# Token chunks of 512, 512 and 128 in place of three of 384 in the gate and merge products of a hybrid encoder step

## The chip, the cores and the metric

The kernel runs on one core of a Trainium2 chip. The metric is the device time of one execution in microseconds (us). The profile comes from one execution of its own, whose time stands in the table below beside its span, which runs from the first to the last instruction.

Engines are named as the profile names them: PE is TensorE's matmul, PEld its weight load, DVE VectorE, ACT ScalarE, POOL GpSimd, SP SyncE, which issues the transfers. All matrix products that matter here have 32-bit operands in the format `float32r` (fp32r in the rows of ACT and DVE; the rows of PE print it as f32, as they do for plain 32-bit floats).

## What is computed

One layer of a streaming encoder, for 1024 new tokens behind 16 learned meta tokens and for 8 running streams of 16 tokens, model width 1024. The input projection gives ten parts of 1024 columns; attention has 8 heads of 128. Cut to the parts that the change touches:

```
xn = rmsnorm(x, norm_g);  p = xn @ w_in + b_in
B, C, h, z_c, q, k, v, z_s, g_c, g_s = split(p)
y_c = silu(z_c) * (B * causal_conv3(C * h))
y_s = silu(z_s) * stick_breaking(q, k, v)
m   = sigmoid(g_c) * (y_c @ w_conv_o) + sigmoid(g_s) * (y_s @ w_sb_o)
y   = x + m @ w_o
```

The meta tokens need no output, so everything from the gates on covers 1152 tokens: 1024 of the prompt and 128 of the running streams.

## The kernel before

Activations lie turned, 128 channels on the partitions and tokens along the free axis. A weight matrix is taken in tiles of 1024 input channels by 128 output channels. For near-32-bit accuracy both operands of a product are split in a high and a low part in fp32r, and `split_product` (L64) issues three matmuls for each of the 8 blocks of 128 input channels: high by high (L70), low activation or low weight (L71, L72). A weight tile therefore needs 24 matmuls for each chunk of tokens, and each of these matmuls has a weight load of 128 columns of its own. A chunk fills one PSUM bank, of which 384 of the 512 columns are used; three chunks, `CHL` (L48), cover the 1152 tokens, so a tile takes 72 matmuls.

The program is four stages, one behind the other, each engine with a program written out by hand and semaphores between them:

- the front: norm, then the short convolution, eight blocks of four weight tiles (`conv_chunk`, L385; its first two tiles use chunks of 400, 384 and 384 tokens, since they hold the meta tokens too, the other two `CHL`)
- the gates (`two_blocks`, L438 on PE, L527 on ACT, the loop at L651 on DVE): eight blocks of three weight tiles, g_c, then y_c @ w_conv_o, then g_s. Chunk n goes into bank `g_banks[n]` (L246). ACT takes sigmoids out of the banks (L538, L548), DVE multiplies (L656), and both results go to memory
- attention, eight heads
- merge and output (`merge_and_output`, L1472), over `LIVE_CHUNKS` (L49): eight tiles of w_sb_o, in which DVE multiplies (L1603), adds (L1605) and takes the low part (L1596) while ACT takes the high part (L1569); then eight tiles of w_o, whose result ACT copies out (L1579), PE turns back (L1655) and DVE adds to x (L1616)

`LIVE_CHUNKS` also cuts the last head's output at the seam between attention and merge (L1348, L1437, L1444). The gates of the attention heads (`silu_gate`, L1039) use `CHL`.

PE waits for a weight tile (`ready`) and, before each chunk, until the chunk before it in the same bank has been read. Weight tiles are loaded two ahead, split by ACT (L148) and POOL (L153) after the product that used the slot.

Of the kernel before, what the change touches and what calls it, by code (L numbers as in the profile page):

```python
# [34 lines left out]
META, SEQ, NB, DS, PAST = 16, 1024, 8, 16, 512  # L35
HEADS, HD = 8, 128
PT = SEQ // P
SAMPLE0 = META + SEQ
TOK = SAMPLE0 + NB * DS
# [6 lines left out]
OFF = {n: i * D for i, n in enumerate(["B", "C", "h", "z_c", "q", "k", "v", "z_s", "g_c", "g_s"])}  # L46
CH = [(0, META + 384), (META + 384, META + 768), (META + 768, TOK)]
CHL = [(META, META + 384), (META + 384, META + 768), (META + 768, TOK)]  # L48
LIVE_CHUNKS = [(a - META, e - META) for a, e in CHL]  # L49


def tile_cols(t):
# [47 lines left out]
def hold(eng, sem, value):  # L100


    eng.wait_ge(sem, value)
    eng.sem_inc(HELD["waits_held"], 1)
# [59 lines left out]
def x_moving(c, c0, c1):  # L164
    return (lambda k: c.xh[:, k, c0:c1], lambda k: c.xl[:, k, c0:c1])
# [8 lines left out]
def front(c, d):  # L174
# [81 lines left out]
    def bias(name, i):  # L256
        return c.bias[:, bass.ds(i + OFF[name] // P, 1)]
# [114 lines left out]
    def tensor(pe):  # L372
        def turn(p):

            n = rows[p]
            pe.wait_ge(normed, p + 1)
            for j in range(2):
                if p >= 2:
                    pe.wait_ge(lo_ok, 2 * (p - 2) + j + 1)
                for k in range(4):  # L380
                    mm = pe.transpose(x_banks[p % 2][j][:, k * P:k * P + n],
                                      xn[0:n, p % 3, (4 * j + k) * P:(4 * j + k + 1) * P], c.ident[0:n, 0:n])
                mm.then_inc(turned, 1)

        def conv_chunk(i, j, n, ks=range(KC)):  # L385
            c0, c1 = (CH if names[j] in "Ch" else CHL)[n]
            q = 3 * j + n
            if q < 2:
                pe.wait_ge(d_out, 9 * i + q + 1)
            elif q < 5:  # L390
                pe.wait_ge(c_out, 3 * i + q - 1)
            else:
                pe.wait_ge(d_out, 9 * i + q - 4 + 2)
            mm = w.product(pe, j, banks[q % 2][:, 0:c1 - c0], x_moving(c, c0, c1), ks)
            if KC - 1 in ks:
                mm.then_inc(full, 1)

        pe.wait_ge(made, 4)
        pe.wait_ge(gain_in, 16)
        for j in range(2):  # L400
            mm = pe.matmul(c.bank_z[:, j * 512:(j + 1) * 512], ones[:, :], gb[:, j * 512:(j + 1) * 512],
                           start=True, stop=True)
        mm.then_inc(gain_ok, 1)
        for p in range(TILES):
            turn(p)
            if p == 4:
                pe.wait_ge(small_in, 48)
                pe.transpose(small_bank[:, 0:80], b80[:, :], c.ident[0:80, 0:80])
                for k in range(KC):
                    pe.transpose(small_bank[:, 80 + 3 * k:83 + 3 * k], cw3[:, k * P:(k + 1) * P], c.ident[0:3, 0:3])  # L410
                for k in range(KC):
                    mm = pe.transpose(small_bank[:, 128 + 16 * k:144 + 16 * k], st16[:, k * P:(k + 1) * P],
                                      c.ident[0:16, 0:16])
                mm.then_inc(small_turned, 1)
            if p in C_HALVES:

                n, ks = C_HALVES[p]
                if n == 0:
                    w.ready(pe, 0, 0)
                pe.wait_ge(lo_ok, 2 * CHUNK_TILES[n])  # L420
                conv_chunk(0, 0, n, ks)
        pe.wait_ge(lo_ok, 2 * CHUNK_TILES[2])
        conv_chunk(0, 0, 2)
        for j in range(1, 4):
            w.ready(pe, 0, j)
            for n in range(3):
                conv_chunk(0, j, n)
        with pe.Fori(1, KC) as i:
            for j in range(4):
                w.ready(pe, i, j)  # L430
                for n in range(3):
                    conv_chunk(i, j, n)
        pe.wait_ge(last_ok, 2 * KC)
        for k in range(KC):
            mm = pe.transpose(c.bank_z[0:18, k * P:(k + 1) * P], last[:, k, :], c.ident[:, :])
        mm.then_inc(last_turned, 1)

        def two_blocks(i, first):  # L438
            for j in range(6):
                b = 2 * i + j // 3  # L440
                wg.ready(pe, i, j)
                for n, (c0, c1) in enumerate(CHL):
                    if j % 3 == 0:
                        if first and j == 0 and n == 2:
                            pe.wait_ge(last_out, 1)
                        pe.wait_ge(s_ok, 3 * b + n + 1)
                    elif j % 3 == 1:
                        if first and j == 1 and n == 0:
                            pe.wait_ge(yl_ok, 3 * KC)
                        pe.wait_ge(g_ok, 3 * b + n + 1)  # L450
                    else:
                        pe.wait_ge(m_ok, 3 * b + n + 1)
                    right = x_moving(c, c0, c1) if j % 3 != 1 else (
                        lambda k: yh[:, k, c0 - META:c1 - META], lambda k: yl[:, k, c0 - META:c1 - META])
                    wg.product(pe, j, g_banks[n][:, 0:c1 - c0], right).then_inc(g_full, 1)

        two_blocks(0, True)
        with pe.Fori(1, KC // 2) as i:
            two_blocks(i, False)

    def scalar(act, first_splits):
# [65 lines left out]
        def two_blocks(i, more):  # L527
            for b in range(2):
                m = 2 * i + b

                def split(j):
                    if b == 0 or more or j < 3:
                        jj = 3 * b + j
                        wg.split_hi(act, *((i, jj) if jj < 6 else (i + 1, jj - 6)))

                for n, (c0, c1) in enumerate(CHL):
                    hold(act, g_full, 9 * m + n + 1)
                    act.activation(gate[:, c0 - META:c1 - META], g_banks[n][:, 0:c1 - c0], ACT.Sigmoid,  # L538
                                   bias=bias("g_c", m)).then_inc(g_ok, 1)
                split(2)  # L540
                act.wait_ge(g_full, 9 * m + 6)
                split(3)
                if b and not more:
                    first_splits(act)
                act.wait_ge(s_stored, 16 * m + 16)
                for n, (c0, c1) in enumerate(CHL):
                    hold(act, g_full, 9 * m + 6 + n + 1)
                    act.activation(outs[:, 1, c0 - META:c1 - META], g_banks[n][:, 0:c1 - c0], ACT.Sigmoid,  # L548
                                   bias=bias("g_s", m)).then_inc(s_ok, 1)
                split(4)  # L550

        act.wait_ge(yl_ok, 3 * KC)
        with act.Fori(0, KC // 2 - 1) as i:
            two_blocks(i, True)
        two_blocks(KC // 2 - 1, False)

    def vector(dve):
# [35 lines left out]
        with dve.Fori(0, KC) as i:  # L593
            dve.tensor_copy(us[:, :, 0:2], state[:, bass.ds(i, 1), :].rearrange("p o (b j) -> p (o b) j", j=2)
                            ).then_inc(u_ok, 1)
            for n, (c0, c1) in enumerate(CH):
# [3 lines left out]
                e = min(c1, SAMPLE0)  # L600
# [35 lines left out]
            for n, (c0, c1) in enumerate(CHL):  # L636
                q = 9 + n
                a, b = c0 - META, c1 - META
# [11 lines left out]

        with dve.Fori(0, KC) as i:  # L651
            dve.wait_ge(m_stored, 16 * i + 16)
            for n, (c0, c1) in enumerate(CHL):
                dve.wait_ge(g_full, 9 * i + 3 + n + 1)
                dve.wait_ge(g_ok, 3 * i + n + 1)
                dve.tensor_tensor(outs[:, 0, c0 - META:c1 - META], g_banks[n][:, 0:c1 - c0],  # L656
                                  gate[:, c0 - META:c1 - META], ALU.mult).then_inc(m_ok, 1)
# [16 lines left out]
    done.y_c_used, done.stored = y_c_used, all_stored  # L674
    done.conv_banks_read, done.gate_banks_read = conv_banks_read, gate_banks_read
    return Programs(sync, gpsimd, tensor, scalar, vector), done


# [79 lines left out]
def attention(c, d, buf, front_stored, following):  # L758
# [51 lines left out]
    def turn_bank(h, plan, key):  # L810

        n = plan[key]
        return FIRST_T + NT * h + n, c.bank_t[n % 2]
# [395 lines left out]
    def scalar(act):  # L1209
# [88 lines left out]
        def head(h, par, pairs, nxt, nxt2):  # L1298
# [48 lines left out]
            else:  # L1347
                for n, (a, e) in enumerate(LIVE_CHUNKS):  # L1348
                    act.wait_ge(y_ok, HEADS + n)
# [15 lines left out]
    def vector(dve):  # L1365
# [53 lines left out]
        def head(h, par, pairs, nxt, nxt2):  # L1419
# [16 lines left out]
            dve.wait_ge(t_out, turn_bank(h, plan, ("o", 1))[0] + 1 + 2)  # L1436
            for a, e in [(0, LIVE)] if nxt else LIVE_CHUNKS:  # L1437
                dve.tensor_tensor(ot[:, a:e], zs[:, a:e], ot[:, a:e], ALU.mult).then_inc(y_ok, 1)
# [4 lines left out]
            else:  # L1443
                for n, (a, e) in enumerate(LIVE_CHUNKS):  # L1444
                    dve.wait_ge(yh_ok, HEADS + n)
# [26 lines left out]
def merge_and_output(c, d, e):  # L1472
# [26 lines left out]
    turn_banks = [c.bank_t[0], c.bank_t[1], c.bank_z[:, 0:512]]  # L1499
    chunks = LIVE_CHUNKS  # L1500

# [300 lines left out]
```

## Time and profile before

| | |
|---|---|
| median of 3 executions | 1709.81 us (1708.9 to 1711.69) |
| the profiled execution | 1708.88 us, of it span 1707.1 us |
| PE busy | 1669.0 us, 98% of the span |
| DVE, ACT, POOL busy | 572.7, 516.2, 360.2 us |
| gates | about 437 to 738 us of the span |
| merge, output | about 1491 to 1592, 1592 to 1707 us |

A matmul's record begins when it starts in the array and ends when its last result is out, so records of a dense stream overlap: what one costs is the distance between the starts of neighbours, not the length of a record. Two passes of one plain 32-bit product are two records.

### The profile page before, as it was taken

Reading aid. Unit: us, or ns where it says so; the run is one execution under the profiler, and the core shown is the slowest. Engines: PE = TensorE matmul, PEld = TensorE weight load, DVE = VectorE, ACT = ScalarE, POOL = GpSimd, SP = SyncE. Lnnn points to the kernel's source line nnn. Section 1 sums busy time; section 2 is a strip of 40 time slices with the busy share of each in tenths; the row PEclk is TensorE's granted clock in tenths of the full one; section 3 lists DMA queues with packets and bytes.
Section 4 is the critical chain, followed back from the end, with each engine's and each line's share of the span. In section 5 each row is a group of like instructions: output and inputs, shape, how many; then the busy total and the mean of one; then the engine's idle time right before and its main releaser. Section 6 shows DMA issues by size and latency. Waiting matters only on the chain.

```text
span 1707.1 us, 27313 instructions
## 1 busy us (share of the span) xinstructions
PE 1669.0 (98%) x10845; PEld 1592.3 (93%) x10845; DVE 572.7 (34%) x912; ACT 516.2 (30%) x1225; POOL 360.2 (21%) x334
## 2 busy tenths in 40 slices
PE   7999999999999999999999999999999998699998
PEld 6999999999999999998999899898989897499998
DVE  5433323433200000023444343535343534544211
ACT  6211222211211111124434343434353533511111
POOL 3211212211212112132121212112121210511111
PEclk9999999999999999999999999999999999799999
DMA  5111111101222212243242423333242223434244
GB/s 165 46 30 49 48 38 37 45 29 49 65 67 79 77 65 71 83 137 92 68 117 66 119 74 97 99 89 104 83 104 76 66 63 100 157 122 157 52 129 119
DMA packets 227891, 142.15 MB, mean 83 GB/s; under 512 B 8150, under 2 KB 220710, under 8 KB 227804
## 3 DMA queue, kind: packets, MB, share of 16 engines
q1 hardware_dynamic: 227804, 140.94, 28.5%
q8 instruction: 61, 1.00, 0.2%
q14 instruction: 26, 0.21, 0.0%
HBM read 112.98 MB, written 27.93 MB: 83 GB/s over the span
## 4 chain that ended last, share of the span: by engine, by line
PE 94%; ACT 2%; DMA 1%; issue 1%; DVE 1%; POOL 1%; SPq 0%; DVEq 0%; ACTq 0%; POOLq 0%
PE bank_p L70 18%; PE bank_p L71 18%; PE bank_p L72 18%; PE bank_o L1116 4%; PE bank_z L1064 4%; PE bank_o L71 3%; PE bank_o L70 3%; PE bank_o L72 3%; PE bank_z L71 3%; PE bank_z L70 3%; PE bank_z L72 3%; PE bank_t L1105 2%; PE bank_s L71 2%; PE bank_s L70 2%; PE bank_s L72 2%; PE bank_t L1077 2%
## 5 line engine op out<-in xcount | busy, mean ns | idle before, releaser
L70 PE MATMUL bank_p<-x_hi,w_hi 128*128 128x384 f32 (+1 forms) x768 | 262.1, 341 | 2.1 <-DVE x_lo L571 1.4
L72 PE MATMUL bank_p<-x_hi,w_lo 128*128 128x384 f32 (+1 forms) x768 | 260.4, 339 | 0.0
L71 PE MATMUL bank_p<-x_lo,w_hi 128*128 128x384 f32 (+1 forms) x768 | 260.2, 339 | 0.0
L153 POOL TENSOR_TENSOR w_lo<-w_raw,w_hi 128x1024 fp32r<-128x1024 f32 x56 | 139.5, 2490 | 551.7 <-ACT w_hi L148 551.7
L70 PE MATMUL bank_p<-wqkv_hi,x_hi 128*128 128x384 f32 (+1 forms) x640 | 218.3, 341 | 0.0
L72 PE MATMUL bank_p<-wqkv_hi,x_lo 128*128 128x384 f32 (+1 forms) x640 | 211.7, 331 | 0.0
L71 PE MATMUL bank_p<-wqkv_lo,x_hi 128*128 128x384 f32 (+1 forms) x640 | 211.5, 330 | 0.0
L70 PEld LDWEIGHTS bank_p<-x_hi,w_hi 128*128 128x128 f32 x768 | 144.2, 188 | 4.3 <-DVE x_lo L571 2.6
L72 PEld LDWEIGHTS bank_p<-x_hi,w_lo 128*128 128x128 f32 x768 | 144.2, 188 | 0.0
L71 PEld LDWEIGHTS bank_p<-x_lo,w_hi 128*128 128x128 f32 x768 | 144.0, 188 | 0.0
L1395 DVE TENSOR_TENSOR_SCAN one_minus_beta<-one_minus_beta 128x1040 f32<-128x1040 f32 (+8 forms) x72 | 116.1, 1613 | 49.0 <-ACT one_minus_beta L1233 49.0
L962 POOL TENSOR_SCALAR qk_meansq<-qk_sumsq 128x2 f32<-128x2 f32 x80 | 15.3, 191 | 502.9 <-ACT squares L1214 502.9
L71 PEld LDWEIGHTS bank_p<-wqkv_lo,x_hi 128*128 128x128 f32 (+1 forms) x640 | 114.5, 179 | 1.3
L70 PEld LDWEIGHTS bank_p<-wqkv_hi,x_hi 128*128 128x128 f32 (+1 forms) x640 | 114.3, 179 | 1.1
L72 PEld LDWEIGHTS bank_p<-wqkv_hi,x_lo 128*128 128x128 f32 (+1 forms) x640 | 114.1, 178 | 1.3
L148 ACT ACTIVATE w_hi<-w_raw 128x1024 fp32r<-128x1024 f32 x56 | 59.1, 1055 | 166.2 <-PE bank_p L72 89.9
L1385 DVE SCALAR_TENSOR_TENSOR qk_rows<-qk_rows,qk_rstd,qk_gain 128x128 f32<-128x128 f32 (+1 forms) x152 | 63.8, 459 | 119.7 <-POOL qk_rstd L964 119.7
L1116 PE MATMUL bank_o<-a_turned,v_rows 128*128 128x128 f32 x576 | 80.9, 278 | 0.0
L1064 PE MATMUL bank_z<-qk_turned 128*128 128x512 f32 (+1 forms) x192 | 78.6, 519 | 1.7 <-ACT beta L1233 1.7
L1376 DVE TENSOR_TENSOR qk_rows<-bank_p,bias_qkv 128x256 f32<-128x256 f32 x80 | 32.8, 410 | 137.6 <-PE bank_p L72 135.8
L656 DVE TENSOR_TENSOR gates_out<-bank_o,gate_c 128x384 f32<-128x384 f32 x8 | 4.5, 558 | 211.9 <-PE bank_o L72 211.9
L153 POOL TENSOR_TENSOR wm_lo<-wm_raw,wm_hi 128x1024 fp32r<-128x1024 f32 x16 | 41.2, 2579 | 161.4 <-ACT wm_hi L148 161.4
(232 smaller groups left out, 3449.9 us busy)
## 6 DMA issues: line engine op xcount, KB each, us to landing
w_raw<-in_w_in SPq DMA_DIRECT2D x48, 512.0 KB, 3.8
cache_k_rows<-in_cache_k SPq DMA_DIRECT2D x64, 256.0 KB, 3.8
cache_v_rows<-in_cache_v SPq DMA_DIRECT2D x64, 256.0 KB, 4.6
wqkv_raw<-in_w_in SPq DMA_DIRECT2D x24, 512.0 KB, 5.3
m_part_scratch<-gates_out SPq DMA_DIRECT2D x8, 576.0 KB, 2.8
gate_scratch<-gates_out SPq DMA_DIRECT2D x8, 576.0 KB, 2.8
gate_s<-gate_scratch SPq DMA_DIRECT2D x8, 576.0 KB, 3.9
m_part<-m_part_scratch SPq DMA_DIRECT2D x8, 576.0 KB, 5.0
```

What stands on the lines that cost most here:

```text
L70: pe.matmul(out, lh(k), rh(k), start=k == 0, stop=False)
L71: pe.matmul(out, lh(k), rl(k), start=False, stop=False)
L72: mm = pe.matmul(out, ll(k), rh(k), start=False, stop=k == KC - 1)
L148: act.activation(self.hi[:, s, :, :], self.raw[:, s, :, :], ACT.Copy).then_inc(self.hi_ok, 1)
L153: pool.tensor_tensor(self.lo[:, s, :, :], self.raw[:, s, :, :], self.hi[:, s, :, :].bitcast(F32), ALU.subtract).then_inc(self.lo_ok, 1)
L1064: pe.matmul(c.bank_z[:, a:e], q, qk[:, par, 1, skip + a:skip + e], start=True, stop=e < w)
L1077: mm = pe.transpose(bank[:, q * P:(q + 1) * P], kc[:, j % 2, q, :], c.ident[:, :])
L1105: mm = pe.transpose(bank[0:n, m * P:(m + 1) * P], src, c.ident[:, :])
L1116: mm = pe.matmul(c.bank_o[:, 0:P], v[:, par, t, :], a, start=g == 0 and m == 0, stop=g == len(groups) - 1 and m == len(groups[g]) - 1)
L1376: dve.tensor_tensor(qkn[0:n, s, a:2 * P], bank[0:n, a:2 * P], bias3[0:n, a:2 * P], ALU.add).then_inc(rows_ok, 1)
L1385: mm = dve.scalar_tensor_tensor(out=qkn[0:n, s, j * P:(j + 1) * P], in0=qkn[0:n, s, j * P:(j + 1) * P], scalar=rs[0:n, s, j:j + 1], in1=ga ...
L1395: dve.tensor_tensor_scan(young_first, young_first, young_first, 1.0, ALU.mult, ALU.bypass).then_inc(scan_ok, 1)
```

## The change

A new list `WIDE` cuts the 1152 tokens in two chunks of 512 and one of 128. The gate products and what reads their banks take it in place of `CHL`, and `LIVE_CHUNKS` follows from it, so that the merge and output products and the seam behind the last head are cut in the same way. `CHL` itself stays for the convolution and for the attention heads' gates. The number of chunks, the banks, the semaphores and their counts stay as they were.

```diff
-LIVE_CHUNKS = [(a - META, e - META) for a, e in CHL]
+WIDE = [(META, META + 512), (META + 512, SAMPLE0), (SAMPLE0, TOK)]
+LIVE_CHUNKS = [(a - META, e - META) for a, e in WIDE]
...
                 wg.ready(pe, i, j)
-                for n, (c0, c1) in enumerate(CHL):
+                for n, (c0, c1) in enumerate(WIDE):
...
-                for n, (c0, c1) in enumerate(CHL):
+                for n, (c0, c1) in enumerate(WIDE):
                     hold(act, g_full, 9 * m + n + 1)
...
-                for n, (c0, c1) in enumerate(CHL):
+                for n, (c0, c1) in enumerate(WIDE):
                     hold(act, g_full, 9 * m + 6 + n + 1)
...
             dve.wait_ge(m_stored, 16 * i + 16)
-            for n, (c0, c1) in enumerate(CHL):
+            for n, (c0, c1) in enumerate(WIDE):
                 dve.wait_ge(g_full, 9 * i + 3 + n + 1)
```

The four loops are those of PE's gate matmuls, of ACT's sigmoids of g_c and of g_s, and of DVE's multiply.

On PE, in the first gate tile, the end of the second chunk and the start of the third (x_hi and x_lo are the activations' parts, w_hi and w_lo the weights'; the last number is the tokens). Before:

```order
L72 MATMUL bank_s<-x_hi,w_lo 128x384
L70 MATMUL bank_z<-x_hi,w_hi 128x384
L71 MATMUL bank_z<-x_lo,w_hi 128x384
L72 MATMUL bank_z<-x_hi,w_lo 128x384
L70 MATMUL bank_z<-x_hi,w_hi 128x384
```

and in the changed kernel, whose lines stand one further down:

```order
L73 MATMUL bank_s<-x_hi,w_lo 128x512
L71 MATMUL bank_z<-x_hi,w_hi 128x128
L72 MATMUL bank_z<-x_lo,w_hi 128x128
L73 MATMUL bank_z<-x_hi,w_lo 128x128
L71 MATMUL bank_z<-x_hi,w_hi 128x128
```

The order of the matmuls and their number are the same; 24 in a row now have 128 columns each.

On DVE, in the last merge tile before the output stage (gate_s is the gate, m_part the sum so far, m_lo the low part that PE reads in the output stage). Before:

```order
L1603 TENSOR_TENSOR gate_s<-bank_z,gate_s 128x384
L1604 REGISTER_ALU
L1605 TENSOR_TENSOR m_part<-m_part,gate_s 128x384
L1596 ISA
L1596 TENSOR_TENSOR m_lo<-m_part,m_hi 128x384
L1602 REGISTER_ALU
L1603 TENSOR_TENSOR gate_s<-bank_s,gate_s 128x384
```

and in the changed kernel:

```order
L1604 TENSOR_TENSOR gate_s<-bank_z,gate_s 128x512
L1605 REGISTER_ALU
L1606 TENSOR_TENSOR m_part<-m_part,gate_s 128x512
L1597 ISA
L1597 TENSOR_TENSOR m_lo<-m_part,m_hi 128x512
L1603 REGISTER_ALU
L1604 TENSOR_TENSOR gate_s<-bank_s,gate_s 128x128
```

Nothing moved; the work on the second chunk is a third longer, that on the last a third of what it was.

## Rows read from the trace of the kernel before

**Rows 1.** The page: engines' busy time, and the chain that ended last

```profile
PE 1669.0 (98%) x10845; PEld 1592.3 (93%) x10845; DVE 572.7 (34%) x912; ACT 516.2 (30%) x1225; POOL 360.2 (21%) x334
...
PE 94%; ACT 2%; DMA 1%; issue 1%; DVE 1%; POOL 1%; SPq 0%; DVEq 0%; ACTq 0%; POOLq 0%
```

**Rows 2.** Busy time of engines in stretches of gates, merge (first line: columns)

```profile
core 0: us, PE busy (x) PEld busy (x) DVE busy (x) ACT busy (x) POOL busy (x), PEclk, DMA share, GB/s
444.00:727.00 283.00, 283.00 (x1624) 283.00 (x1623) 13.51 (x25) 47.87 (x68) 53.30 (x25) 1.00 0.23 74
1491.00:1592.00 101.00, 101.00 (x576) 101.00 (x575) 51.39 (x75) 21.25 (x34) 18.88 (x7) 1.00 0.47 148
```

**Rows 3.** One line's instructions, L656: durations, first and last start

```profile
L656 DVE TENSOR_TENSOR gates_out<-bank_z,gate_c x8: 557/558/559, 462.9 to 726.6; 128x384 f32<-128x384 f32 x8
```

**Rows 4.** PE's groups by shape: count | busy us, mean ns of one | idle before

```profile
L72 PE MATMUL bank_p<-x_hi,w_lo 128*128 128x384 f32 x640 | 216.2, 338 | 0.0
L71 PE MATMUL bank_p<-x_lo,w_hi 128*128 128x384 f32 x640 | 216.1, 338 | 0.0
...
L71 PE MATMUL bank_p<-wqkv_lo,x_hi 128*128 128x384 f32 x576 | 193.8, 336 | 0.0
...
L72 PE MATMUL bank_p<-x_hi,w_lo 128*128 128x400 f32 x128 | 44.2, 345 | 0.0
L71 PE MATMUL bank_p<-x_lo,w_hi 128*128 128x400 f32 x128 | 44.1, 345 | 0.0
...
L71 PE MATMUL bank_p<-wqkv_lo,x_hi 128*16 128x256 f32 x64 | 17.7, 277 | 0.0
```

**Rows 5.** Timeline of PE in attention: start us, length us, neighbours merged (xcount)

```profile
883.36 0.22 PE L1065 MATMUL bank_z<-mask,ident_bf 128*128 128x128 bf16 x1
883.41 0.35 PE L1070 MATMUL bank_t<-qk_turned 128*128 128x16 f32 x2
```

**Rows 6.** The same stretch on PEld, the weight loads

```profile
882.93 0.10 PEld L1065 LDWEIGHTS bank_z<-mask,ident_bf 128*128 128x128 bf16 x1 [0.24 <-issue]
883.36 0.30 PEld L1070 LDWEIGHTS bank_t<-qk_turned 128*128 128x128 f32 x2 [0.33 <-issue]
```

**Rows 7.** L1070's instructions: ns min/median/max of one

```profile
L1070 PEld LDWEIGHTS bank_t<-qk_turned x32: 190/191/192, 793.0 to 1459.5; 128*128 128x128 f32 x32
L1070 PE MATMUL bank_t<-qk_turned x32: 235/248/263, 793.1 to 1459.5; 128*128 128x16 f32 x32
```

**Rows 8.** PEld's groups by shape: a gate weight, a bf16 weight

```profile
L70 PEld LDWEIGHTS bank_o<-x_hi,w_hi 128*128 128x128 f32 x128 | 24.0, 188 | 0.0
...
L1065 PEld LDWEIGHTS bank_z<-mask,ident_bf 128*128 128x128 bf16 x64 | 6.4, 99 | 7.1 <-issue 4.5
```

**Rows 9.** Timeline of PE, value products of plain 32-bit operands

```profile
896.63 1.06 PE L1116 MATMUL bank_o<-a_turned,v_rows 128*128 128x128 f32 x8
```

**Rows 10.** L1116's matmuls: ns min/median/max of one

```profile
L1116 PE MATMUL bank_o<-a_turned,v_rows x576: 275/275/421, 805.5 to 1490.8; 128*128 128x128 f32 x192
```

**Rows 11.** Timeline of ACT in a gate tile [idle before it, who ended that]

```profile
483.87 0.58 ACT L538 ACTIVATE gate_c<-bank_s,bias_turned 128x384 f32<-128x384 f32 x1 [3.54 <-PE bank_s L72]
488.07 0.58 ACT L538 ACTIVATE gate_c<-bank_z,bias_turned 128x384 f32<-128x384 f32 x1 [3.62 <-PE bank_z L72]
488.55 1.05 ACT L148 ACTIVATE w_hi<-w_raw 128x1024 fp32r<-128x1024 f32 x1
```

**Rows 12.** Timeline of POOL in the same stretch

```profile
489.68 2.40 POOL L153 TENSOR_TENSOR w_lo<-w_raw,w_hi 128x1024 fp32r<-128x1024 f32 x1 [10.20 <-ACT w_hi L148]
```

**Rows 13.** Timeline of DVE at the end of the merge

```profile
1588.39 0.56 DVE L1603 TENSOR_TENSOR gate_s<-bank_z,gate_s 128x384 f32<-128x384 f32 x1 [3.08 <-PE bank_z L72]
1588.98 0.56 DVE L1605 TENSOR_TENSOR m_part<-m_part,gate_s 128x384 f32<-128x384 f32 x1
1589.45 0.55 DVE L1596 TENSOR_TENSOR m_lo<-m_part,m_hi 128x384 f32 x1
```

**Rows 14.** Timeline of PE there: last merge and first output matmul

```profile
1592.24 0.34 PE L72 MATMUL bank_s<-x_hi,wm_lo 128*128 128x384 f32 x1
1592.41 0.33 PE L70 MATMUL bank_p<-m_hi,wm_hi 128*128 128x384 f32 x1
```

## The prediction

> **What bounds the kernel now.** I read the page first: PE is busy 98% of the span and makes up 94% of the chain that ended last, while DVE, ACT and POOL stand at 34, 30 and 21% [rows 1]. Then I looked at the stretches that the change touches, since an average over the program proves nothing about them. In the gates and in the merge PE is busy in every microsecond, at the full granted clock (1.00, the 2.4 GHz level), with DVE and ACT far below it [rows 2]. So each nanosecond that a matmul of these stages gains or loses goes straight into the time, and nothing that shortens DVE or ACT gives anything back. The question is the price of one matmul, taken from starts, since records overlap.
>
> That price now: DVE multiplies out of bank_z once per gate block, right behind PE's product; its first and its eighth start are 726.6 − 462.9 = 263.7 us apart [rows 3]. That is seven blocks of 3 tiles × 72 matmuls, so 174.4 ns for one matmul.
>
> **The change part by part.** It touches 40 weight tiles: 8 × 3 in the gates, 8 of w_sb_o, 8 of w_o. A tile goes from 72 matmuls of 384 columns to 48 of 512 and 24 of 128. Columns (1152) and weight loads (72) are the same in sum.
>
> *A tile before:* 72 × 174.4 = 12,557 ns.
>
> *The 512-wide matmuls.* The latency in a record is the same for every width, so the difference of mean records is the price of columns: 345 − 338 ns for 400 against 384 columns [rows 4], 7 ns for 16. A rounded difference of 7 over 16 columns is coarse, 0.4 to 0.5 ns a column; 1/2.4 GHz, the level that the rows show as granted, is 0.417 and lies within it. I take that: 174.4 + 128 × 0.417 = 227.8 ns. Of the 174.4 ns, 160 are columns and some 14 come on top of them per matmul. If that extra vanished, 512 columns would cost 213.5. From the other side, 256 to 384 columns takes 336 − 277 = 59 ns [rows 4], 0.461 a column (the 256-wide ones load weights of only 16 columns), which gives 174.4 + 59 = 233.4. The value taken is the step between two rows with equal weight loads.
>
> *The 128-wide matmuls.* No fp32r matmul in this trace is narrower than 256 columns, so this is the open price. By columns alone it is 128 × 0.417 = 53.4 ns, below everything else a matmul needs. What a full-width stretch hides is the load of the next weights: one load per 174.4 ns fits easily there, and a 128-wide matmul may be too short a cover. The nearest row on a load's price is L1070: two matmuls of only 16 columns, each with its own load of 128 columns of 32-bit weights. Their columns are nearly nothing, yet the two records together last 350 ns [rows 5] where the first alone is 235 [rows 7], so the ends lie 350 − 235 = 115 ns apart; the two loads last 300 ns together [rows 6] and 190 each [rows 7], so they start 110 apart. These are plain 32-bit weights, but the record of a gate's fp32r weight is as long, 188 ns, while a bf16 weight shows 99 [rows 8]. A dense stream of 128-wide plain 32-bit matmuls, each with a load, agrees: (1060 − 275) / 7 = 112 ns from start to start [rows 9, 10]. I take 112. The ends: 53.4 below; above, the price of a plain 32-bit product of this width, two such passes, 224.
>
> *A tile after:* 48 × 227.8 + 24 × 112 = 10,934 + 2,688 = 13,622 ns, 1,065 more than before. Forty tiles: +42.6 us.
>
> *Everything around it costs nothing.* ACT's and DVE's reads of a bank get a third longer or shorter: 0.58 us becomes some 0.75, behind idle times of 3.5 us and more [rows 11]. Weight splits: after g_c's last sigmoid at 488.07 ACT and POOL need until 489.68 + 2.40 = 492.08 [rows 11, 12], and the tile is wanted one tile (now 13.6 us) later. A slower PE gives all of this more room. The one place where DVE stands before PE is the merge's end: the first output chunk needs m_lo of the first chunk, which DVE makes behind the second chunk's product, in 1589.45 + 0.55 − 1588.39 = 1.61 us; PE wants it at 1592.41 [rows 13, 14], 2.4 us later. After the change the cover is the narrow run, 24 × 112 = 2.7 us, against 1.61 × 512/384 = 2.1 us. It just holds; without cover (narrow at 53.4 ns, 1.3 us) it would cost 0.8 us once. At the seam behind the last head, 21 wider matmuls cover the last split; no gain there, since PE does not wait.
>
> *Sum.* The profiled execution took 1708.9 us: 1708.9 + 42.6 = 1751.5. The median of the runs is 0.9 above it, so I write 1752.
>
> With 213.5 and with 233.4 for the wide ones the same sum gives +15 and +53 us: 1725 and 1763. The low one needs the extra to vanish wholly, which the step from 384 to 400 doesn't show; for a bare load of 110 ns and an extra that shrinks by half, 1735 or so is as low as this mechanism goes.
>
> **The rivals.** All keep 227.8 for the wide ones.
>
> *Narrow matmuls cost their columns (faster).* PE pulls the next loads far enough ahead. For it: a bf16 matmul of 128 columns starts only 883.41 − 883.36 = 0.05 us before its successor [rows 5]. Against it: bf16 loads have half as long a record [rows 8], and L1070's matmuls wait for theirs. The point that decides is (12,557 − 10,934) / 24 = 67.6 ns: below it the kernel gets faster. At 55 ns the tile takes 12,254 ns and the whole 12 us less: 1698. Just at 68 ns, by columns with the same extra of 14, nothing changes: 1710. That the change is not in the program is no rival; the order shows 512 and 128.
>
> *Loads hide in part.* Halfway between 55 and 112, 84 ns: 24 × (84 − 67.6) × 40 = +16 us, 1726. The Trainium skill, "TensorE: Matmul & The Clock Gate", section "Back-to-back issue gap", gives about 81 ns for a 128-column matmul in a stream of load and matmul pairs; by that figure, as an estimate, the narrow run would add 13 us (1723). The same passage has 131 ns for 512 columns, by which the change would save far more; this trace speaks against it, since 384 columns already take 174.4 ns [rows 3].
>
> *fp32r loads are dearer than plain ones.* They can't be dearer than 174.4, for today's stream does one in that time. At this end: 10,934 + 24 × 174.4 = 15,120, +2,563 a tile, +102 us: 1812. Against it: the equal records [rows 8].
>
> *A narrow fp32r matmul loses its single-pass rate* and costs what plain 32-bit products cost, 224 ns: 10,934 + 5,376 = 16,310, +3,753 a tile, +150 us: 1860. For it: nothing narrower than 256 in this trace shows that the rate holds. Against it: the 256-wide rows are at full rate [rows 4], no sign of a decline.
>
> **How the numbers follow.** Load-bound narrow run at 1735 to 1765: 0.74. Dearer fp32r loads, between 1765 and 1812: 0.07. Loss of the single pass, near 1860: 0.10. Loads hidden in part, near 1725: 0.03. Columns alone, near 1698: 0.04. No change: 0.02. The first two make 0.81, so the range is 1735 to 1812. A measurement can tell about 0.2%, 3.4 us, from no change: faster 0.04, same 0.02, slower 0.94.
>
> **What would show it.** In the gates, bank_z products of neighbouring blocks should lie 3 × 13.62 = 40.9 us apart where they were 37.7. A run of 24 narrow matmuls should last 2.7 us; 1.3 to 1.6 would mean hidden loads, 5.4 the loss of the single pass. The wide records should be 338 + 53 = 391 ns, 397 at the upper end. PE must stay free of waits in gates and merge, and the clock at its upper level. If PE waits at the merge's end, or if the clock falls in the half-empty narrow runs, the sum is short of a term. A time under 1735 with narrow gaps of 112 would mean that the wide price was wrong; over 1812, that narrow fp32r matmuls cost something this trace doesn't show.

## The result and the profile after

| | before | after |
|---|---|---|
| median, us | 1709.55 | 1758.23 |
| ratio (95% interval) | | 1.028 (1.0263 to 1.0298) |
| profiled execution, us | 1708.88 | 1758.83 |
| its span, us | 1707.1 | 1757.0 |

The change makes the kernel slower by 48.7 us. The forecast was 1752 us, with a range of 1735 to 1812: direction, mechanism and range held, and the loss is 6 us larger than the 42.6 us of the sum.

The page of the changed kernel, busy time by engine and then the chain that ended last by engine; they answer to [rows 1]:

```profile
PE 1718.4 (98%) x10845; PEld 1559.3 (89%) x10845; DVE 575.1 (33%) x912; ACT 514.4 (29%) x1225; POOL 357.6 (20%) x334
...
PE 95%; ACT 2%; DMA 1%; issue 1%; DVE 1%; POOL 1%; SPq 0%; DVEq 0%; ACTq 0%; POOLq 0%
```

PE's busy time grew by as much as the span did, and the chain is PE even more than before. The busy times in three windows of after answer to [rows 2]: the gates, the merge and the output stage (columns: window and sum, then busy us of PE, PEld, DVE, ACT and POOL with instruction counts, granted clock, DMA share, GB/s):

```profile
444.00:750.00 306.00, 306.00 (x1589) 258.25 (x1588) 13.47 (x24) 48.29 (x68) 52.84 (x22) 1.00 0.22 69
1524.00:1612.00 88.00, 88.00 (x457) 74.34 (x456) 44.07 (x61) 16.79 (x28) 14.37 (x6) 1.00 0.39 127
1640.00:1740.00 100.00, 100.00 (x555) 86.75 (x554) 8.91 (x18) 15.60 (x27) 14.28 (x6) 1.00 0.33 92
```

PE is busy in every microsecond, at a granted clock of 1.00 (the 2.4 GHz level), narrow runs included. The list of PE's waits is empty for the gates and for merge and output (but for 0.3 us at the very end, which stand there before and after alike). So no wait and no fall of the clock was added: the same count of matmuls takes longer.

What a weight tile costs is read, as in [rows 3], from instructions that follow the last bank of a tile: DVE's gate product (gates), DVE's second product (merge) and ACT's turning read (output). These are groups of after with minimum, median and maximum in ns, first and last start in us, then shapes:

```profile
L657 DVE TENSOR_TENSOR gates_out<-bank_z,gate_c x8: 291/292/292, 467.7 to 759.1; 128x128 f32<-128x128 f32 x8
L1604 DVE TENSOR_TENSOR gate_s<-bank_o,gate_s x4: 290/291/291, 1537.8 to 1620.6; 128x128 f32<-128x128 f32 x4
L1580 ACT ACTIVATE y_turned<-bank_o x8: 277/277/278, 1648.0 to 1749.0; 128x128 f32<-128x128 f32 x8
```

and the same groups of before, for the two stages whose rows do not stand ahead of the prediction:

```profile
L1603 DVE TENSOR_TENSOR gate_s<-bank_o,gate_s x4: 558/558/558, 1503.9 to 1579.9; 128x384 f32<-128x384 f32 x4
L1579 ACT ACTIVATE y_turned<-bank_o x8: 492/493/494, 1605.1 to 1699.1; 128x384 f32<-128x384 f32 x8
```

Dividing the stretch from first to last start by the tiles in it gives the price of a tile:

| stage | tiles in the stretch | before, us | after, us | tiles of the stage | added, us |
|---|---|---|---|---|---|
| gates | 21 | 263.7/21 = 12.557 | 291.4/21 = 13.876 | 24 | 24 × 1.319 = 31.7 |
| merge | 6 | 76.0/6 = 12.667 | 82.8/6 = 13.800 | 8 | 8 × 1.133 = 9.1 |
| output | 7 | 94.0/7 = 13.429 | 101.0/7 = 14.429 | 8 | 8 × 1.000 = 8.0 |

(A tile of the output stage holds PE's transposes too, before and after alike.) The sum is 48.8 us, the difference of the medians (48.7). The two profiled spans lie 49.9 us apart; the 1.1 us left over is less than the spread of the runs of the kernel before (1708.9 to 1711.7 us). Where the time sits inside a tile is seen in the timeline of PE: start in us, length in us, engine, line, operation. First the narrow run behind the wide ones, in the gates:

```profile
464.60 0.40 PE L73 MATMUL bank_s<-y_c_hi,w_lo 128*128 128x512 f32 x1
464.83 0.22 PE L71 MATMUL bank_z<-y_c_hi,w_hi 128*128 128x128 f32 x1
464.89 0.27 PE L72 MATMUL bank_z<-y_c_lo,w_hi 128*128 128x128 f32 x1
465.00 0.28 PE L73 MATMUL bank_z<-y_c_hi,w_lo 128*128 128x128 f32 x1
...
467.34 0.27 PE L73 MATMUL bank_z<-y_c_hi,w_lo 128*128 128x128 f32 x1
467.46 0.44 PE L71 MATMUL bank_o<-x_hi,w_hi 128*128 128x512 f32 x1
467.74 0.40 PE L72 MATMUL bank_o<-x_lo,w_hi 128*128 128x512 f32 x1
```

From 465.00 to 467.34 there are 21 steps: (467.34 − 465.00)/21 = 111 ns each, twice the 53.3 ns of the columns. The first narrow one follows a wide one, and its successor starts 60 ns later; the wide one behind the run takes 50 ns more than others. The run as a whole costs what 24 loads cost.

The wide matmuls, in the output stage, nine steps:

```profile
1641.78 0.39 PE L71 MATMUL bank_p<-m_hi,wm_hi 128*128 128x512 f32 x1
...
1643.82 0.39 PE L71 MATMUL bank_p<-m_hi,wm_hi 128*128 128x512 f32 x1
```

2.04 us for nine: 227 ns, as forecast. In the gates it is another figure:

```profile
516.06 0.40 PE L71 MATMUL bank_s<-x_hi,w_hi 128*128 128x512 f32 x1
...
518.16 0.40 PE L71 MATMUL bank_s<-x_hi,w_hi 128*128 128x512 f32 x1
```

2.10 us for nine: 233 ns. The price of a tile says the same: with 24 × 112 = 2,688 ns for the narrow run, (13,876 − 2,688)/48 = 233.1 ns are left for a wide one. The mean records by shape (busy us, mean ns, idle us before) show it too: 389 ns in the output stage, 395 in the gates.

```profile
L72 PE MATMUL bank_s<-x_lo,w_hi 128*128 128x512 f32 x128 | 50.6, 395 | 0.0
L72 PE MATMUL bank_p<-m_lo,wm_hi 128*128 128x512 f32 x128 | 49.8, 389 | 0.0
```

Two questions are left to test. Is the narrow price really a floor set by the weight load, and why did the wide price come out 5 ns too high in the gates and not in the output stage?

### The profile page after: what moved, and what is told of

The parts are those of the page before. It is cut to its first block, busy times and chain, and to the rows that moved or that the text cites. A ratio compares the mean times of both kernels' runs of the same rounds, so it can differ in the third digit from the quotient of the medians.

```text
span 1757.0 us, 27313 instructions
## 1 busy us (share of the span) xinstructions
PE 1718.4 (98%) x10845; PEld 1559.3 (89%) x10845; DVE 575.1 (33%) x912; ACT 514.4 (29%) x1225; POOL 357.6 (20%) x334
## 4 chain that ended last, share of the span: by engine, by line
PE 95%; ACT 2%; DMA 1%; issue 1%; DVE 1%; POOL 1%; SPq 0%; DVEq 0%; ACTq 0%; POOLq 0%
PE bank_p L71 18%; PE bank_p L73 18%; PE bank_p L72 18%; PE bank_o L1117 4%; PE bank_z L1065 4%; PE bank_o L71 3%; PE bank_o L73 3%; PE bank_o L72 3%; PE bank_s L73 3%; PE bank_s L72 3%; PE bank_s L71 3%; PE bank_t L1106 2%; PE bank_z L72 2%; PE bank_z L73 2%; PE bank_z L71 2%; PE bank_t L1078 2%
## 5 line engine op out<-in xcount | busy, mean ns | idle before, releaser
L71 PE MATMUL bank_p<-x_hi,w_hi 128*128 128x384 f32 (+1 forms) x768 | 262.9, 342 | 0.7 <-ACT c_part L500 0.7
L71 PE MATMUL bank_p<-wqkv_hi,x_hi 128*128 128x384 f32 (+1 forms) x640 | 218.2, 341 | 0.0
L71 PEld LDWEIGHTS bank_p<-x_hi,w_hi 128*128 128x128 f32 x768 | 144.8, 189 | 2.7 <-DVE conv_out L635 1.6
L1396 DVE TENSOR_TENSOR_SCAN one_minus_beta<-one_minus_beta 128x1040 f32<-128x1040 f32 (+8 forms) x72 | 116.2, 1614 | 48.7 <-ACT one_minus_beta L1234 48.7
L71 PEld LDWEIGHTS bank_p<-wqkv_hi,x_hi 128*128 128x128 f32 (+1 forms) x640 | 114.3, 179 | 1.1
L657 DVE TENSOR_TENSOR gates_out<-bank_o,gate_c 128x512 f32<-128x512 f32 x8 | 5.5, 692 | 244.6 <-PE bank_o L73 244.6
```

The source lines that it names most:

```text
L71: pe.matmul(out, lh(k), rh(k), start=k == 0, stop=False)
L1396: dve.tensor_tensor_scan(young_first, young_first, young_first, 1.0, ALU.mult, ALU.bypass).then_inc(scan_ok, 1)
```

## The experiments

The theory: a matmul that loads 128 columns of 32-bit weights cannot follow its predecessor sooner than one load takes, some 112 ns, whatever its width. The rivals: the price is two passes over the columns (128 × 2 / 2.4 = 107 ns looks alike at this one width), or it depends on the run of narrow matmuls standing in a row. Ratios stand against the kernel before on the same chip.

### e1_w480: 480, 480 and 192

```diff
-WIDE = [(META, META + 512), (META + 512, SAMPLE0), (SAMPLE0, TOK)]
+WIDE = [(META, META + 480), (META + 480, META + 960), (META + 960, TOK)]
```

> Chunks of 480, 480 and 192 tokens in place of 512, 512 and 128, otherwise the changed kernel. Theory (a narrow matmul costs the load of the next weights, 112 ns, whatever its width below some 230 columns): the narrow run stays at 24 x 112 = 2.7 us though its matmuls are half as wide again. With wide ones at 213 to 219 ns a tile is 12.9 to 13.2 us, 0.4 to 0.6 more than in the kernel before, so 16 to 26 us in all: 1725 to 1736 us. Rival (below some width an fp32r matmul pays twice per column, which for 128 columns is about 107 ns too): narrow ones at 160 to 165 ns, a tile 14.2 to 14.5 us, 1775 to 1787 us.

Measured: 1729.88 us, ratio 1.0126 (1.0110 to 1.0143). The narrow run in the timeline of PE:

```profile
461.01 0.27 PE L73 MATMUL bank_z<-y_c_hi,w_lo 128*128 128x192 f32 x1
...
463.36 0.28 PE L73 MATMUL bank_z<-y_c_hi,w_lo 128*128 128x192 f32 x1
```

21 steps, 2.35 us: 112 ns, with half as many columns again as in the changed kernel. The price does not move with the columns, so two passes (160 ns at this width) are out, and the floor stands. DVE's gate product gives the tile:

```profile
L657 DVE TENSOR_TENSOR gates_out<-bank_z,gate_c x8: 357/358/358, 463.8 to 739.4; 128x192 f32<-128x192 f32 x8
```

275.6/21 = 13.124 us, 0.567 over before, where after has 1.319.

### e2_w448: 448, 448 and 256

```diff
-WIDE = [(META, META + 512), (META + 512, SAMPLE0), (SAMPLE0, TOK)]
+WIDE = [(META, META + 448), (META + 448, META + 896), (META + 896, TOK)]
```

> Chunks of 448, 448 and 256 tokens. Theory (floor of one load, 112 ns): 256 columns at 0.417 ns and some 13 ns on top take 120 ns, above the floor, so nothing is paid any more: the time of the kernel before, 1700 to 1716 us. Rival (twice per column for narrow ones): 256-wide matmuls at 213 ns or more, +90 us, 1800 us; if the doubling sets in only below 256, this run can't tell it from the theory.

Measured: 1709.34 us, ratio 1.0003 (0.9994 to 1.0013): no difference from before. The narrow run:

```profile
461.42 0.28 PE L73 MATMUL bank_z<-y_c_hi,w_lo 128*128 128x256 f32 x1
...
463.89 0.28 PE L73 MATMUL bank_z<-y_c_hi,w_lo 128*128 128x256 f32 x1
```

2.47/21 = 117.6 ns for 106.7 ns of columns: columns set the price again, and the uneven split is free. The corner lies where the columns with their extra reach the load: (112 − 14) × 2.4 = 235 columns, an estimate from the 174.4 − 160 = 14 ns of [rows 3] and the 112 ns measured; with the 117.6 − 106.7 = 11 ns of this run it is 243. 192 columns lie under it and cost time, 256 lie over it and cost none.

### e3_half_load: half the load under the same columns

In the narrow matmuls only the first 64 of 128 output channels are loaded and computed.

```diff
-        return split_product(pe, out, (lambda k: self.hi[:, s, k, :], lambda k: self.lo[:, s, k, :]), right, ks)
+        m = 64 if right[0](0).shape[-1] == 128 else P
+        return split_product(pe, out[0:m, :], (lambda k: self.hi[:, s, k, 0:m], lambda k: self.lo[:, s, k, 0:m]), right, ks)
```

> The changed kernel, but the 128-wide matmuls load only 64 of the 128 weight columns (the other half of the output channels of the sample tokens is left out). They still move 128 columns. Theory (load bound): half a load is about 56 ns, now below the 67 ns that the columns take; the narrow run falls from 2.7 to 1.6 us and the whole from 1758 to about 1715 us. Rival (the moved columns or the kind of product set the price): the narrow run stays at 2.7 us, 1758 us.

Measured: 1711.77 us, ratio 1.0018 (1.0008 to 1.0027). With columns, width and order untouched, some 46 of the 48.7 us are gone. The narrow run:

```profile
461.42 0.22 PE L71 MATMUL bank_z<-y_c_hi,w_hi 128*64 128x128 f32 x1
461.48 0.22 PE L72 MATMUL bank_z<-y_c_lo,w_hi 128*64 128x128 f32 x1
...
462.80 0.22 PE L73 MATMUL bank_z<-y_c_hi,w_lo 128*64 128x128 f32 x1
```

From the first to the last row 1.38 us for 23 steps: 60 ns, the columns' 53.3 and some 7 more. So the 112 ns of a 128-column matmul go with the weight load. (Half of the output channels went with it, but e1 wrote half as many columns again at the same price.) The time came out 3 us under the expectation of 1715, which had taken 67 ns for a narrow matmul: 7 ns less each are 7 × 24 × 40 = 6.7 us. Two things take part of that back. The wide matmul behind the run still loads 128 columns under a narrow one: it starts at 462.86 and its successor at 463.14 us, 0.28 later instead of 0.23, 40 × 0.05 = 2.0 us. The other 0.8 us are a wait.

That wait belongs to a term which the prediction had put at nothing. The list of PE's waits of e3 in the merge and output stages shows it, and neither before nor after has it (us in total, times, longest):

```profile
PE bank_p L71 <- DVE m_lo L1598: 0.8, 1, 0.8
```

The prediction named this wait and its price: "without cover (narrow at 53.4 ns, 1.3 us) it would cost 0.8 us once". With the narrow run at 24 × 60 = 1.4 us the cover is gone, and it costs 0.8 us once.

### e4_gates_only: the change in the gates alone

```diff
-LIVE_CHUNKS = [(a - META, e - META) for a, e in WIDE]
+LIVE_CHUNKS = [(a - META, e - META) for a, e in CHL]
```

> WIDE in the gates alone, merge and output with chunks of 384 as before. Theory (a price per tile, 24 of 40 tiles): the gates keep their 31.6 us, the rest goes back: 1741 us. Rival (part of the loss is a seam between stages or a wait behind the attention): merge and output don't give back their 17 us, 1745 to 1758 us.

Measured: 1740.08 us, ratio 1.0187 (1.0170 to 1.0204), against 1741 expected. The two groups, gates as after and merge as before:

```profile
L657 DVE TENSOR_TENSOR gates_out<-bank_z,gate_c x8: 291/292/292, 465.5 to 756.8; 128x128 f32<-128x128 f32 x8
L1604 DVE TENSOR_TENSOR gate_s<-bank_o,gate_s x4: 557/558/558, 1533.2 to 1609.3; 128x384 f32<-128x384 f32 x4
```

291.3/21 = 13.871 us and 76.1/6 = 12.683 us a tile. 24 tiles cost 31 us and the other 16 the rest: a price per tile, which adds up, and no event at a seam.

### e5_alternate: narrow matmuls between wide ones

In the gates, the second wide chunk and the narrow one take turns, matmul by matmul, so that each narrow one has a wide one on either side.

```diff
...
+                    if n == 0:
+                        wg.product(pe, j, bank_of(0), right_of(0)).then_inc(g_full, 1)
+                s = j % wg.slots
+                for k in range(KC):
+                    for p in range(3):
+                        for n in (1, 2):
+                            left = (wg.lo if p == 2 else wg.hi)[:, s, k, :]
+                            last_one = k == KC - 1 and p == 2
+                            mm = pe.matmul(bank_of(n), left, right_of(n)[1 if p == 1 else 0](k),
+                                           start=k == 0 and p == 0, stop=last_one)
...
```

> The changed kernel, but in the gates the second 512-wide and the 128-wide chunk of a tile alternate matmul by matmul, so that a narrow one never follows a narrow one. Theory (only the one next load runs ahead, so behind every narrow matmul a full load stands open): the pair costs 233 + 112 ns as before, the whole stays at 1755 to 1762 us. Rival (loads run several matmuls ahead, and only a long narrow run exhausts them): the pair costs 233 + 67 ns, the gates lose 24 tiles x 24 x 45 ns = 26 us, 1732 us.

Measured: 1756.47 us, ratio 1.0282 (1.0265 to 1.0299): as slow as after. The timeline of PE:

```profile
500.52 0.22 PE L472 MATMUL bank_z<-y_c_hi,w_hi 128*128 128x128 f32 x1
500.58 0.45 PE L472 MATMUL bank_s<-y_c_lo,w_hi 128*128 128x512 f32 x1
500.86 0.22 PE L472 MATMUL bank_z<-y_c_lo,w_hi 128*128 128x128 f32 x1
500.92 0.44 PE L472 MATMUL bank_s<-y_c_hi,w_lo 128*128 128x512 f32 x1
```

A pair takes 0.34 us (500.52 to 500.86), the sum of 228 to 233 for a wide one and some 110 for a narrow one. A wide matmul of 230 ns has time for two loads of 110, yet nothing is hidden: the next wide one starts 60 ns after the narrow one and then needs 0.28 us instead of 0.23. The weight loads of the same stretch show why:

```profile
500.52 0.19 PEld L472 LDWEIGHTS bank_s<-y_c_lo,w_hi 128*128 128x128 f32 x1
500.63 0.19 PEld L472 LDWEIGHTS bank_z<-y_c_lo,w_hi 128*128 128x128 f32 x1
500.87 0.19 PEld L472 LDWEIGHTS bank_s<-y_c_hi,w_lo 128*128 128x128 f32 x1
```

The wide one's load begins with the narrow matmul, at 500.52, and the next load 0.11 us later. The load after that begins only at 500.87, with the next narrow matmul (500.86), though the loader was through with the one before by some 500.74 (500.63 + 0.11). In these rows loads run no more than one matmul ahead; under a narrow matmul there is only 53 ns of cover for the load of its successor, and the rest shows. Taking turns with wide ones doesn't mend it.

The Trainium skill, "TensorE: Matmul & The Clock Gate", section "LDWEIGHTS (loading the stationary operand)", gives a load's price as its number of columns over 1.2 GHz. By it, as an estimate, 128 columns would be 107 ns and 64 would be 53. The traces come near the first with 111 to 112, and for the second e3 shows 60, where the columns (53.3 ns) are as long anyway.

### What the wide ones cost: e6 to e9

The 5 ns per wide matmul that the sum lacked are there in the gates (233) and not in the output stage (227), with the same shape, dtype and load. The other engines don't make the difference. In the two stretches shown above, of the gates and of the output stage, DVE, ACT and POOL have no instruction at all (columns as in the windows above):

```profile
516.06:518.16 2.10, 2.10 (x10) 1.70 (x9) 0.00 (x0) 0.00 (x0) 0.00 (x0) 1.00 0.04 13
1641.78:1643.82 2.04, 2.04 (x11) 1.69 (x9) 0.00 (x0) 0.00 (x0) 0.00 (x0) 1.00 0.00 0
```

What differs, besides the bank, are the buffers that the operands lie in. The theory of these four runs: the surplus depends on where an operand lies in SBUF. The rival: it belongs to the width and stays when buffers move.

**e6_shift_y** moves the y_c operands of the gates by 64 bytes, **e7_shift_w** the gate weights (and the front's) by 32:

```diff
-            c.sb(conv, "room_for_w3", [P, 1000])
+            c.sb(conv, "room_for_w3", [P, 1016])
```

> The changed kernel, with the buffers of y_c (the moving operand of the middle gate product) 64 bytes further on in SBUF; all else in place. In question is the term that the prediction sized too small: y_c's 512-wide matmuls take 234 ns from start to start, where 384 and 448 wide ones take 173 and 200, which with 0.417 ns a column would make 227. Theory (where operands lie in SBUF sets the surplus): y_c's wide matmuls change, to 227 to 231 ns or to another value; those of x in the gates stay at 232 to 233. Rival (the surplus belongs to the width 512 in these stages): y_c stays at 234. The time moves by at most 8 x 48 x 7 ns = 2.7 us either way.

```diff
+        c.sb(ctx, "pad", [P, 8])
         w = WeightTiles(c, ctx, "w", 2, 4)
...
-            c.sb(conv, "room_for_w3", [P, 1000])
+            c.sb(conv, "room_for_w3", [P, 992])
```

> The changed kernel, with the weight tiles of front and gates 32 bytes further on (they start 32 bytes past a multiple of 64 now, then on one; y_c stays where it was). Theory (operands' places in SBUF set the surplus): x's and y_c's wide matmuls in the gates change from 232 to 234 ns towards 227, worth 24 x 48 x 6 ns = 7 us, and the front's 384-wide ones from 177 towards 173, worth up to 2304 x 4 ns = 9 us: 1742 to 1758 us. Rival (the width): no change, 1758 us.

Measured: 1758.13 us for e6 (a single run) and 1757.24 us (ratio 1.0280, 1.0263 to 1.0297) for e7. One group of wide records (minimum/median/maximum in ns) in after, e6 and e7, in this order:

```profile
L72 PE MATMUL bank_s<-y_c_lo,w_hi x64: 392/396/400, 459.4 to 755.7; 128*128 128x512 f32 x64
```

```profile
L72 PE MATMUL bank_s<-y_c_lo,w_hi x64: 395/396/397, 459.5 to 755.0; 128*128 128x512 f32 x64
```

```profile
L72 PE MATMUL bank_s<-y_c_lo,w_hi x64: 390/393/404, 456.7 to 751.8; 128*128 128x512 f32 x64
```

The medians move by 0 and 3 ns, with no return to the 389 of the output stage. These two didn't find a place that sets it, and by themselves they spoke for the rival.

**e8_before_shift_w** puts the same 32 bytes into the kernel before (the chunks are 384 again):

```diff
+        c.sb(ctx, "pad", [P, 8])
         w = WeightTiles(c, ctx, "w", 2, 4)
...
-            c.sb(conv, "room_for_w3", [P, 1000])
+            c.sb(conv, "room_for_w3", [P, 992])
```

> The kernel before, chunks of 384, with the same shift of the weight tiles by 32 bytes. Theory (places): the front's 384-wide matmuls go from 177 towards 173 ns and x's in the gates from 175 to 173, up to 9 + 2 us: 1698 to 1709 us. Rival: no change, 1709 us.

Measured: 1711.58 us, ratio 1.0014 (1.0004 to 1.0023), a little slower. DVE's gate product:

```profile
L657 DVE TENSOR_TENSOR gates_out<-bank_z,gate_c x8: 557/557/557, 463.3 to 729.3; 128x384 f32<-128x384 f32 x8
```

266.0/21 = 12.667 us a tile where before has 12.557; 24 × 0.11 = 2.6 us, which covers the 2.3 us measured against before on the same chip (1709.25). From trace to trace the stretch from first to last start repeats more closely than that: 291.4 us in after, 291.3 in e4. So the price of an unchanged 384-wide matmul moves with an unused 32 bytes ahead of its weights: 12,667/72 = 175.9 ns against 174.4. It moved the other way than expected: the theory had 1698 to 1709 us.

**e9_shift_wm** does the same to the stage that was cheap: the merge and output weights of after go 32 bytes on, what lies behind them 128.

```diff
+        c.sb(ctx, "pad_wm", [P, 8])
         e.w = WeightTiles(c, ctx, "wm", 2, 2)
+        c.sb(ctx, "pad_wm2", [P, 24])
```

> The changed kernel, with the weight tiles of merge and output 32 bytes further on in SBUF and what is allocated behind them (the low part of m among it) 128 bytes further on. In the output stage the 512-wide matmuls take 227 ns, which is 384's 173.3 and 128 columns at 0.417; in the gates and the merge they take 232 to 234. Theory (operands' places decide whether there is a surplus on top): the output's wide ones rise to 229 to 235 ns, the time by up to 8 x 48 x 6 ns = 2.3 us. Rival (place plays no part at this width; it is something else of the stage): they stay at 227.

Measured: 1761.68 us (a single run). The wide records of the output stage by shape, a wide run in the timeline, and ACT's turning read, all of e9:

```profile
L72 PE MATMUL bank_p<-m_lo,wm_hi 128*128 128x512 f32 x128 | 50.7, 396 | 0.0
```

```profile
1650.25 0.40 PE L71 MATMUL bank_p<-m_hi,wm_hi 128*128 128x512 f32 x1
...
1651.65 0.40 PE L71 MATMUL bank_p<-m_hi,wm_hi 128*128 128x512 f32 x1
```

```profile
L1580 ACT ACTIVATE y_turned<-bank_o x8: 278/278/278, 1649.0 to 1751.9; 128x128 f32<-128x128 f32 x8
```

1.40 us for six: 233 ns where after has 227, the record 396 where it was 389, and 102.9/7 = 14.70 us a tile instead of 14.43. The cheap stage has become as dear as the gates by moving buffers alone. m_hi lies ahead of what was moved and kept its place, yet its matmuls (L71) became dearer as well, so the weights' move has a part in it. In the merge, which reads the same moved weights, nothing changed: DVE's second product has 82.9 us from first to last start, where after has 82.8. So the places of the operands set a surplus in the output stage (e9) and move the price at 384 columns (e8); there the rival falls. For the gates at 512 columns it isn't shown: e6 and e7 tried two places and moved the records by 0 to 3 ns. Which rule of addresses decides, and whether a place exists at which the gates' wide matmuls cost 227, stays open.

## Why the prediction was right, and where it was off

- **PE as the bound, no new wait.** Right: PE fills the windows, no waits, clock at its upper level.
- **The narrow price, 112 ns.** Right to a nanosecond, and it is the step that carries the verdict. It had been taken from plain 32-bit matmuls and a load's record; e1 and e3 show that it is the load, e5 that the neighbours' width doesn't hide it. The four rivals on it (columns alone, hidden in part, dearer loads, loss of the single pass) are all out by the 111 ns steps. The Trainium skill, "TensorE: Matmul & The Clock Gate", section "Back-to-back issue gap", has 81 ns for this width and 131 for 512 columns; here it is 112 and 227 to 233, so the measurement decides against both.
- **The wide price, 227.8 ns.** The mis-sized term. Measured: 227 in the output stage, 233 in the gates. The merge's tile of 13,800 ns gives (13,800 − 2,688)/48 = 231.5. The gates' 24 tiles came out at 1.319 us each against 1.065 forecast, 24 × 0.254 = 6.1 us, and that is the miss; merge and output were off by +0.5 and −0.5 us. The step that failed added columns at 1/2.4 GHz to the price at 384, as though what comes on top were fixed. It isn't: e8 and e9 show it to depend on where operands lie. Nor is it the same at every width: in the gates it is 11 ns at 256 columns (117.6 − 106.7, e2), 14 at 384 (174.4 − 160) and 20 at 512 (233.1 − 213.3), while the output stage has 14 at 512 (227 − 213.3). The records say the same: from 384 to 512 columns the mean of one product grew from 337 to 395 ns in the gates (x_lo, bank_s), 58 ns, and from 335 to 389 in the output stage (m_lo, bank_p), 54 ns, where 128 columns are 53. Whether the width does that in the gates, or the places at which chunks of another width begin, no run separates. The upper bound named, 233.4, was the value that held in the gates, though it had been got from a row with another load; that it fits to 0.3 ns is luck. The forecast for records, 391 with 397 at the upper end, met 389 in the output stage and 395 in the gates: both readings had been there.
- **The blocks' distance.** 40.9 us were forecast, 291.4/7 = 41.6 measured.
- **Everything around it at nothing.** Right in after, where no wait shows; for the merge's end e3 shows the cover and its price of 0.8 us as they had been worked out.

No version beat the kernel before. 448/448/256 ties with it (e2), and the sum of columns gives no reason for more: with 72 loads and 1152 columns a tile in either split, there is nothing to win once every matmul is above the corner.

## What to carry to other kernels

When tokens are split into chunks behind one shared set of weight tiles, look at the narrowest chunk, not at the mean: here each matmul cost the larger of its own columns and the load of its successor's weights, and a narrow one could not borrow cover from the wide ones beside it. With fp32r and 128 weight columns the corner lay between 192 and 256 columns, so a remainder of 256 cost nothing (e2), and a remainder of 128 cost 112 ns for each matmul where its columns take 53. Price a narrow matmul by a load-bound row of the same operand size, and take an extrapolated price of a wide one with a bound of several ns upwards.

## What the runs showed of the hardware that was not expected

- The time on top of the columns is not a fixed price per matmul. In the gates, with the same load of 128 weight columns, it is 11 ns at 256 columns, 14 at 384 and 20 at 512; with 64 weight columns and 128 columns it is 7 (60 − 53.3).
- Moving operands by 32 to 128 bytes changes the price of the same matmul: 174.4 to 175.9 ns at 384 columns (e8), 227 to 233 at 512 in the output stage (e9).
- In e5 a wide matmul behind a narrow one begins in the records 60 ns after it and shows 0.44 us instead of 0.40, and the load of its successor begins 50 ns after that start (500.58 and 500.63): the wait for its weights lies inside its record and not ahead of it, so the list of waits stays empty while PE is held up. A record begins up to 50 ns before its matmul has its weights, and not, as said ahead of the prediction, when the matmul starts in the array. The distances between starts stay the price all the same.
- In e5 a weight load begins no earlier than the matmul just ahead of its own, even where the loader has been free for 0.1 us (500.74 to 500.87).
